# Two transformer blocks on one core: weights of the dilated attention asked for first, neighbourhood tables spread between its units

## What is computed

```python
def second_block(x, ...):
    f = _swiglu(_rmsnorm(x, ffn1_pre_g), ffn1_w_gate, ffn1_w_up, ffn1_w_down)
    x = x + 0.5 * _rmsnorm(f, ffn1_post_g)
    h = _rmsnorm(x, mix_pre_g)
    qa, ka, va, qb, kb, vb, gate_a, gate_b = split(h @ w_in)
    ya = _neighbourhood_attention(qa, ka, va, na_rpb) @ w_branch_a     # scores + a bias gathered from na_rpb
    yb = _dilated_mixture(qb, kb, vb, slopes) @ w_branch_b             # scores - slope * distance
    merged = sigmoid(gate_a) * ya + sigmoid(gate_b) * yb
    x = x + _rmsnorm(merged @ w_out, mix_post_g)
    x = x + 0.5 * _rmsnorm(_swiglu(_rmsnorm(x, ffn2_pre_g), ...), ffn2_post_g)
```

## Time and profile before

| | |
|---|---|
| median of the runs | 3021.47 us (3021.38 to 3021.56) |
| the profiled execution | 3021.78 us |
| its span | 3020.0 us |
| TensorE matmul busy | 2873.5 us, 95% of the span |
| TensorE weight loads busy | 2308.0 us, 76% |
| ScalarE busy | 1259.6 us, 42% |
| GpSimd busy | 1151.2 us, 38% |
| VectorE busy | 1074.5 us, 36% |
| mean granted TensorE clock | 0.98 |
| moved by DMA | 249.85 MB, mean 83 GB/s |

### The profile page before, as it was taken

How to read it: one execution, slowest core, us unless ns; L and a number is a source line. 1 busy time by engine, 2 the same in 40 slices (tenths; PEclk the granted TensorE clock), 3 DMA queues, 4 the chain that set the end, 5 groups by cost and what they waited for, 6 DMA issues and landing times.

```text
span 3020.0 us, 39650 instructions
## 1 busy us (share of the span) xinstructions
PE 2873.5 (95%) x14694; PEld 2308.0 (76%) x14694; DVE 1074.5 (36%) x1401; ACT 1259.6 (42%) x1825; POOL 1151.2 (38%) x296
## 2 busy tenths in 40 slices
PE   7998999999999998999999999999398989999999
PEld 6765688888877764888888888888396768888887
DVE  6254212555122453114553044420204441144421
ACT  5356544555244356345554243331325353343322
POOL 4301255444444100554444444444331324544443
PEclk9999999999999999999999999999799999999999
DMA  5200133333324100342332333322321213323332
GB/s 165 81 12 22 38 101 103 92 97 97 108 89 114 36 1 21 83 126 84 97 97 98 102 97 90 99 95 78 84 84 43 61 36 101 112 82 97 97 102 87
DMA packets 369469, 249.85 MB, mean 83 GB/s; under 512 B 38774, under 2 KB 337478, under 8 KB 369350
## 3 DMA queue, kind: packets, MB, share of 16 engines
q1 hardware_dynamic: 366168, 246.78, 27.3%
q10 hardware_dynamic: 3182, 1.46, 0.2%
HBM read 245.74 MB, written 2.70 MB: 82 GB/s over the span
## 4 chain that ended last, share of the span: by engine, by line
PE 85%; issue 5%; ACT 4%; DVE 2%; POOL 1%; SPq 1%; ACTq 1%; DVEq 0%; DMA 0%; POOLq 0%
PE pair L1498 75%; PE pair L1699 2%; PE pair L1737 1%; PE pair L1720 1%; POOL wlo L498 1%; SPq L457 1%; PE pair L1783 1%; PE pair L1781 1%; DVE sL L1258 1%; ACT tmp L578 1%; PE pair L1769 0%; PE pair L1702 0%; ACT bP L865 0%; DVE hl L1015 0%; ACT tmp L788 0%
## 5 line engine op out<-in xcount | busy, mean ns | idle before, releaser
L498 POOL TENSOR_TENSOR wlo<-raw,whi 128x2048 fp32r<-128x2048 f32 x235 | 1081.4, 4602 | 1844.8 <-ACT whi L542 1844.8
L1498 PE MATMUL pair<-hh,whi 128*128 128x512 f32 (+1 forms) x2256 | 883.2, 391 | 11.5 <-DVE hl L1015 7.7
L1498 PE MATMUL pair<-hl,whi 128*128 128x512 f32 (+1 forms) x2256 | 880.4, 390 | 0.0
L1498 PE MATMUL pair<-hh,wlo 128*128 128x512 f32 (+1 forms) x2256 | 880.3, 390 | 0.0
L542 ACT ACTIVATE whi<-raw 128x2048 fp32r<-128x2048 f32 x235 | 449.4, 1913 | 668.7 <-PE pair L1498 615.0
L1498 PEld LDWEIGHTS pair<-hh,whi 128*128 128x128 f32 (+1 forms) x2256 | 423.7, 188 | 106.1 <-issue 14.4
L1498 PEld LDWEIGHTS pair<-hh,wlo 128*128 128x128 f32 (+1 forms) x2256 | 423.7, 188 | 90.5
L1498 PEld LDWEIGHTS pair<-hl,whi 128*128 128x128 f32 (+1 forms) x2256 | 423.8, 188 | 89.2
L1317 DVE TENSOR_TENSOR a2lo<-tmp,a2hi 128x512 f32 x44 | 200.0, 4546 | 79.4 <-ACT a2hi L851 79.4
L1023 DVE SCALAR_TENSOR_TENSOR pair<-pair,gp_d 128x512 f32<-128x512 f32 x32 | 22.3, 697 | 453.9 <-ACT sq L550 453.7
L1498 PE MATMUL pair<-whi,a1hi 128*128 128x512 f32 x352 | 136.9, 389 | 0.0
(11 more groups left out here) (303 smaller groups left out, 3800.6 us busy)
## 6 DMA issues: line engine op xcount, KB each, us to landing
raw<-in_w_in SPq DMA_DIRECT2D x122, 512.0 KB, 3.9
raw<-in_w_up SPq DMA_DIRECT2D x88, 512.0 KB, 4.3
raw<-in_ffn_w_gate SPq DMA_DIRECT2D x44, 512.0 KB, 3.7
raw<-in_ffn_w_up SPq DMA_DIRECT2D x44, 512.0 KB, 4.7
raw<-in_w_down SPq DMA_DIRECT2D x40, 512.0 KB, 4.5
raw<-in_ffn_w_down SPq DMA_DIRECT2D x40, 512.0 KB, 4.0
raw<-in_w_out SPq DMA_DIRECT2D x24, 512.0 KB, 4.6
raw<-in_w_proj_nsa SPq DMA_DIRECT2D x16, 256.0 KB, 4.0
```

Source lines behind the costliest of these rows:

```text
L498: pool.tensor_tensor(wlo[:, s, :], raw[:, s, :], whi[:, s, :].bitcast(f32), ALU.subtract).then_inc(lo_ready, 1)
L1498: o = pe.matmul(out, l, r, start=start and first, stop=stop and last)
```

## The change

SP's program is written in another order. The units 34 and 35 are asked for ahead of the wait for the end of the down projection. The wait, `cst2` and the wait for `toep_filled` follow in the body of the loop over the dilated units when `u == 1`, and one call of `na_tables` (8 transfers) follows each unit from `u == 1` to `u == 8`. All transfers and all waits of before are still made; the programs of the other engines are the same, with line numbers one higher behind this place.

```diff
--- before.py
+++ after.py
@@ -461,14 +461,15 @@
                     unit(v2 + i, s, twin(A["ffn1_w_gate_2"][0], (2 * i + s) * P, A["ffn1_w_up_2"][0], (2 * i + s) * P, s))
             down(v2 + 11, 0, A["ffn1_w_down_2"][0], A["ffn1_post_g_2"][0], gq_f, A["mix_pre_g_2"][0])
 
-            sp.wait_ge(tile_done, 2 * (DEPTH * UL + 34))
-            sp.dma_start(cst2[:, :], consts2).then_inc(S.const2_in, 16)
-            sp.wait_ge(S.toep_filled, 16)
-            for r in range(8):
-                na_tables(r)
             W = w_in2[0]
             for u, (v, s) in enumerate(DIL_UNITS):
                 unit(v, s, wide(W, 1536 + 768 * (u % 3) + 256 * (u // 3), s))
+                if u == 1:
+                    sp.wait_ge(tile_done, 2 * (DEPTH * UL + 34))
+                    sp.dma_start(cst2[:, :], consts2).then_inc(S.const2_in, 16)
+                    sp.wait_ge(S.toep_filled, 16)
+                if u >= 1:
+                    na_tables(u - 1)
             for u, (v, s) in enumerate(NA_UNITS):
                 unit(v, s, wide(W, (0, 1024, 512)[u // 2] + 256 * (u % 2), s))
             with sp.Fori(0, KT) as m:
```

## The result

The changed kernel took 2975.49 us (median of 2 runs, 2972.65 and 2978.33), against 3021.47 before: a ratio of 0.9848, with a 95% interval of 0.9805 to 0.989. Repeated on another occasion it took 2972.78 (median of 5, 2969.49 to 2974.51) beside 3017.52 for the kernel before, a ratio of 0.9847, now with an interval of 0.9833 to 0.986. The forecast was 2975.7.

What follows compares the result with a forecast made beforehand. TensorE bounds the kernel, with one long hole of 56.48 us. Span 3020.0 less 45.77 is 2974.2; plus 1.8 around the span less 0.3 gives 2975.7 us, other steps and clock at 0; range 2971 to 2982.9.

Steps and rivals of the forecast that it cites:

- The hole: TensorE's wait between the last ffn1 down-projection matmul and the dilated attention's first: 56.48 us, forecast to shrink to 10.71.
- The counterpart in the second layer: Same transition after the first block's second-layer down projection, where weights come in time: 10.71 us, taken as the new length.
- the two levels: Assumed clocks of 2.4 and 1.2 GHz; a granted 0.92 over 86 us means 13.8 us at the lower one.
- SP's wait: SP's wait for the down projection's end, now behind unit 35's request; unit 36's weights still 10.6 to 12.7 us early: 0.
- cst2: A 512 KB transfer, there by 2122.9 at the slowest landing, ahead of ScalarE's asking at 2139.3: cost 0.
- groups behind the weights: Groups 1 to 7 of eight tables follow units 36 to 42: 3.8 us of SP each, cost 0, at worst 30.3 us.
- the last group: Eight tables behind unit 42's weights, there before 2200, first read at 2364.4: cost 0.
- The spare: Time by which dilated weights (unit 40's) land before their conversion: 10.6 us, 8.5 by the slowest landing.
- A: Closing norm before the dilated units still starts late: hole 17.9 us, gain 38.6, 2982.9 us; chance 0.04.
- B: Small table transfers each delay the weights behind them by a 1.8 us landing: 30.1 us returned, 3005.8; chance 0.04.
- C: As B with a higher price: at 3.2 us per landing unit 43 is 115.5 us late, 3091; chance 0.02.
- D: Something other than SP's order holds unit 34's conversion on ScalarE; time stays 3021.5 us; chance 0.01.

Runs made afterwards that it cites:

- by 16: The changed kernel with 16 tables behind each of units 35 to 38 instead of 8 behind each of units 35 to 42: 2972.01 us, ratio 0.9852 to the kernel before.
- by 32: The changed kernel with 32 tables behind each of units 35 and 36 instead of groups of eight: 2975.1 us, ratio 0.986 to the kernel before.

## Why the prediction was right, step by step

**The hole** was forecast to shrink from 56.48 to 10.71 us (9.1 to 11.49) and has 10.88 or 10.92 in all six profiles with the weights in front (the change twice, the block of 64 behind unit 35, by 16, by 32, the block behind unit 42). The counterpart in the second layer was the right row to take; the gain at this place is 45.60 where 45.77 stood. One reading on the way was too strong: the prediction takes all of 2115.9 to 2154.3 as a wait for the 64 tables. They are 30.3 of these 38.4 us, and with none of them ahead of the weights a hole of 26.46 us stays, 15.6 more than with the weights asked for first. The sum did not use this reading, since it took the whole hole from the counterpart.

**The sum.** The span fell by 43.5, not 45.77. Of the difference, 1.33 us lie ahead of the down projection's end, which came at 2116.78 instead of 2115.45 in this execution, 0.17 in the hole, and the remaining 0.8 behind it. One place behind it that differs is the neighbourhood attention. These are the two windows of the neighbourhood attention at the same place in the program, before (first line) and after, with columns as in rows 2:

```profile
2394.00:2444.00 50.00, 44.68 (x283) 30.32 (x281) 29.89 (x86) 25.66 (x65) 9.11 (x2) 0.97 0.18 53
```

```profile
2350.00:2400.00 50.00, 44.68 (x280) 30.57 (x279) 29.41 (x85) 25.52 (x64) 9.12 (x2) 0.93 0.18 53
```

The granted clock is 0.93 where it was 0.97: by the two levels 7 us at 1.2 GHz instead of 3. From the first read of the tables to the last it took 43.5 us instead of 42.9. That the 0.8 us come from this is not shown, and they are no more than the spread: from unit 34's first matmul to the end the changed kernel took 848.84 us in this profile and 847.84 in its other one, the kernel before 848.07. The stretch of the dilated attention, for which the range had 4 us, did not change at all: 0.92 again, and 75.75 us busy of 86 as in the earlier trace rows:

```profile
2220.00:2306.00 86.00, 75.75 (x475) 60.66 (x474) 32.26 (x132) 39.70 (x125) 11.94 (x3) 0.92 0.12 38
```

That the median met the forecast within 0.3 us is thus partly luck, since the two runs behind it are 5.7 us apart. The steadier measure is the gain: 45.77 were forecast, and it was 46.0 the first time and 44.7 the second. The range began at 2971, for which the prediction counted 0.7 of the 1.6 us by which its own bounds let the transition be shorter; two single executions, at 2969.5, lie below it, both medians inside.

**The second to the fifth step** (SP's wait, cst2, groups behind the weights, the last group) were priced at 0, and the waits of TensorE confirm it. Unit 36's request left at 2121.38, 4.2 us behind the wait's end (4.2 forecast), and its conversion followed at 2138.92, right behind a read of PSUM (L875) that had waited 9.40 us for TensorE; the weights held nothing up. The spare was put at 8.5 to 10.6 us, from the distance between request and conversion. This was too small: with groups of 32, 16.7 us of tables stood between the requests of units 36 and 37, and only 2.1 were lost. What the prediction left out of the spare is that TensorE needs the remainder only some 4 us after it is computed (conversion to next unit 10.9, less 1.9 and 4.6). It made no difference to the sum.

**The rivals.** A, the late norm, is what happens with the spreading alone: its chain of 17.6 us was sized rightly, and the change avoids it. B and C, small transfers that add up by their landings, fell with the block of 64 (11.55 us instead of 94) and with the line through 0, 32 and 64. The landing that C asked for even came true and went beyond its 3.2 us, with 3.9 in the changed kernel; by the prediction's formula this would have made unit 43 160 us late, and TensorE waited for no remainder. The Trainium skill's rule (DMA: Bandwidth & Descriptors, Rules for kernel authors), that a transfer under 64 KB is mostly overhead, holds for the single transfer: 24 KB land in 1.8 us, 512 KB in 4.6. The Trainium skill's fixed cost of about 2 us per transfer (same page, Anatomy of one DMA), from which the prediction worked out an estimate, is a fit to transfers issued from GpSimd; these are issued from SP. Read as a price for each transfer of a row, these 2 us would be four times too high; the trace has 0.47. D, that something other than SP's order holds the conversion, fell with the result itself and with the half of the tables ahead.

## What to carry to other kernels

Look at what stands behind a wait in the program of the engine that waits: here 30 us of small transfers made 45 us of idle, because the norm of the stage before was queued behind the conversion of the next stage's weights. Ask a queue for what is needed next ahead of any wait for buffers that it doesn't use, and put small transfers in the gaps in which the queue would wait anyway; a row of them cost its issue time here, not its landings. A transition elsewhere in the same trace, where the weights come in time, is the best measure of what such an edit can give.

## What was not expected

A block of 64 tables took 30.26 us in the kernel before, when all engines stood still, and 31.4 to 31.7 in three kernels where some were at work; why is not shown. In one kernel 32 tables took 15.10 us ahead of the weights and 15.78 behind them. In the changed kernel two of the groups of eight took 4.88 us or more instead of 3.8, with a single issue of 2.1 us. The median landing of a small transfer doubled, from 1.8 to 3.9 us, in groups of eight that follow a large transfer. And single executions of one kernel on one occasion are up to 6.4 us apart (3016.00 to 3022.37 for the kernel before); in the one pair compared, 4.5 of 5.5 us lay in a stretch that no edit here touched. A difference below about 3 us was read from the waits in the trace and not from the times.
